# A router worked in two groups of token tiles, and three weight matrices held until the first gathered rows have landed

## The reference

```python
def hier_moe(hn, w_group, w_expert, w_gate, w_up, w_down):
    t = hn.reshape(-1, d)
    pg = jax.nn.softmax((t @ w_group).astype(jnp.float32), axis=-1)
    g_sel = jnp.argmax(pg, axis=-1)
    ...
    el_sel = jnp.take_along_axis(el, g_sel[:, None, None], axis=1)[:, 0]
    top_p, top_i = lax.top_k(jax.nn.softmax(el_sel, axis=-1), TOP_K_IN_GROUP)
    w = p_sel * top_p / jnp.sum(top_p, axis=-1, keepdims=True)
    ...
    for e in range(N_EXPERTS):
        a = jax.nn.silu(t @ w_gate[e]) * (t @ w_up[e])
        out = out + comb[:, e:e + 1] * (a @ w_down[e]).astype(jnp.float32)
```

## Time and profile before

| | us |
|---|---|
| median of 3 runs | 558.82 |
| lowest, highest | 556.86, 560.46 |
| the profiled execution | 559.13 |
| its span | 557.3 |

### The profile page before, as it was taken

The page is one execution under the profiler, slowest core; times in us unless marked ns, Lnnn a source line. Parts: engine busy times, 40 slices in busy tenths (PEclk is TensorE's granted clock), DMA queues, the critical chain, the costliest instruction groups (busy, mean ns, idle before and its releaser), DMA issues.

```text
span 557.3 us, 7527 instructions
## 1 busy us (share of the span) xinstructions
PE 489.2 (88%) x2747; PEld 309.0 (55%) x2747; DVE 267.8 (48%) x595; ACT 132.7 (24%) x361; POOL 155.8 (28%) x279
## 2 busy tenths in 40 slices
PE   4968989899999989899992999979999789787985
PEld 3946767677776767688882754333433233333333
DVE  2869679878464475752227423223342221122535
ACT  3744455356446223222111100000000000000110
POOL 4354783042113555823004300111112210100003
PEclk9998999799999999899997699989999998898998
DMA  9430220040029703249939989999999999999997
GB/s 296 161 109 23 76 76 2 1 152 1 2 81 319 272 8 98 86 162 411 388 141 403 339 316 376 410 422 417 422 418 420 419 418 420 421 419 421 413 384 268
DMA packets 35030, 144.73 MB, mean 260 GB/s; under 512 B 5842, under 2 KB 8994, under 8 KB 23216
## 3 DMA queue, kind: packets, MB, share of 16 engines
q1 hardware_dynamic: 26320, 129.94, 59.4%
q0 software_dynamic: 4528, 9.01, 4.4%
q10 hardware_dynamic: 4144, 5.28, 2.9%
HBM read 138.16 MB, written 17.30 MB: 279 GB/s over the span
## 4 chain that ended last, share of the span: by engine, by line
PE 38%; DMA 20%; DVE 15%; SPq 11%; issue 6%; ACT 4%; POOL 1%; DVEq 0%; POOLq 0%; ACTq 0%
PE banks L1061 17%; SPq L724 7%; PE banks L1326 5%; DMA y_d<-y_sb,idx 5%; DMA w_moe_b<-in_w_up_dram 5%; DMA y_d<-rows,idx 3%; SPq L732 3%; DMA w_moe_b<-y_d 2%; DMA y_d<-x_row,idx 2%; PE banks L1416 1%; DMA y_sb<-hn_d,idx 1%; PE banks L1276 1%; PE banks L1123 1%; ACT w_hi L1604 1%; PE banks L1341 1%
## 5 line engine op out<-in xcount | busy, mean ns | idle before, releaser
L882 POOL TENSOR_TENSOR w_lo<-w_raw,w_hi 128x512 fp32r<-128x512 f32 x52 | 70.1, 1363 | 113.8 <-ACT w_hi L1604 112.4
L1326 PE MATMUL banks<-w_moe_b,xgT 128*64 128x512 f32 x224 | 68.8, 637 | 10.3 <-DMA w_moe_b<-in_w_up_dram 6.6
L1326 PE MATMUL banks<-w_moe_a,xgT 128*64 128x512 f32 x224 | 67.7, 626 | 5.6 <-DMA w_moe_a<-in_w_up_dram 5.6
L2270 DVE SCALAR_TENSOR_TENSOR glu_b<-banks,wr,glu_a 128x256 f32<-128x256 f32 x15 | 7.2, 483 | 99.5 <-ACT glu_a L1736 99.5
L1736 ACT ACTIVATE glu_a<-banks,wr 128x256 f32<-128x256 f32 x15 | 7.1, 473 | 200.1 <-PE banks L1326 185.7
L1061 PE MATMUL banks<-w_hi,xT_hi_a 128*128 128x512 f32 (+3 forms) x124 | 51.3, 414 | 2.8 <-DVE xT_lo_a L1798 2.8
L1326 PEld LDWEIGHTS banks<-w_moe_b,xgT 128*64 128x64 f32 x224 | 21.7, 145 | 49.8 <-issue 49.1
L1061 PE MATMUL banks<-w_lo,xT_hi_a 128*128 128x512 f32 (+3 forms) x124 | 49.1, 396 | 0.0
L1061 PE MATMUL banks<-w_hi,xT_lo_a 128*128 128x512 f32 (+3 forms) x124 | 48.8, 393 | 0.0
L1326 PEld LDWEIGHTS banks<-w_moe_a,xgT 128*64 128x64 f32 x224 | 21.4, 144 | 27.2 <-issue 27.0
L1061 PE MATMUL banks<-w_hi,xT_hi_b 128*128 128x512 f32 (+3 forms) x92 | 35.7, 388 | 0.4 <-issue 0.4
(11 more groups left out here) (336 smaller groups left out, 910.9 us busy)
## 6 DMA issues: line engine op xcount, KB each, us to landing
w_moe_a<-in_w_down_dram SPq DMA_DIRECT2D x20, 1024.0 KB, 21.0
w_moe_a<-in_w_gate_dram SPq DMA_DIRECT2D x16, 1024.0 KB, 12.4
w_moe_a<-in_w_up_dram SPq DMA_DIRECT2D x16, 1024.0 KB, 14.8
w_moe_b<-in_w_gate_dram SPq DMA_DIRECT2D x14, 1024.0 KB, 18.2
w_moe_b<-in_w_up_dram SPq DMA_DIRECT2D x14, 1024.0 KB, 18.3
w_moe_b<-in_w_down_dram SPq DMA_DIRECT2D x10, 1024.0 KB, 26.5
w_raw<-in_w_in_dram SPq DMA_DIRECT2D x34, 256.0 KB, 4.0
y_d<-in_consts_dram SPq DMA_DIRECT2D x9, 512.0 KB, 10.1
```

The lines of the kernel that those rows point to most:

```text
L882: nc.gpsimd.tensor_tensor(w_lo[:, s, :], w_raw[:, s, :], w_hi[:, s, :].bitcast(F32), ALU.subtract).then_inc(split, 1)
L1326: l = mm(acc[64 * e:64 * e + 64, u, :].rearrange("p (m f) -> p m f", m=2), xgT[:, xu, k, 64 * e:64 * e + 64], units(at_e[e], 2)[:, :, k * ...
L2270: stt(out=glu_b[:, :], in0=acc[:, u, 0:FF], scalar=scales[0], in1=glu_a[:, :], op0=ALU.mult, op1=ALU.mult).then_inc(done, 1)
```

## The change

The router's block is split. The first three tiles of `ORDER` (tile 4, 0 and 1; `AHEAD` = 3) are chosen in a step `choose` that the plan puts between the last jobs of `OUT1`; `logits`, `ssq2` and the table of destinations are now laid out by position in `ORDER`. TensorE's ranks for these three (`ranks_ahead`, three products) stand inside the very last job, ahead of its last matrix; DVE's `rank_in`, `rows_picked` and `rows_placed` stand among the last evictions. The block after the plan does the same for the remaining two tiles: the choice, two products that carry the first group over (one of them with `ahead_sum`) and two more, and rows. `find_rows` for the indices is taken apart: six of its ten products need only the first group. The two steps that make `ms`, and the signal `ms2_rdy` that POOL waits for, move from ahead of the choice to behind the last `row_oh`. One memset of POOL (128 x 768) is dropped, since its memory now serves as scratch.

In SP's queue `gate_v[5]` and `down_v[5]` (pair 2's second expert) and `down_v[0]` move behind the wait for the first gathered rows, where `down_v[1]` already stood.

```diff
@@ -63,6 +63,8 @@
 OUT0 = len(CHUNKS)
 OUT1 = OUT0 + 1
 NJ = NT * (OUT0 + 2)
+AHEAD = 3
+RANK_BANK = 5
...
@@ -185,6 +187,12 @@
             after[s + 1].append(("hT", n, t))
             after[s + 2].append(("logit", n, t))
 
+    last = at[OUT1, ORDER[-1], 0]
+    after[last - 1].append(("choose",))
+    before[last + 1].append(("rank_in",))
+    after[last + 1].append(("rows_picked",))
+    after[last + 2].append(("rows_placed",))
...
@@ -276,7 +288,7 @@
     put("ret_scale", np.concatenate([q_scale, k_scale], -1).transpose(1, 0, 2))
     head = 2 * np.arange(2)[None, :] + (p[:, None] >= 64)
     put("decay", np.stack([gamma[head] ** n for n in (P, DEC, NMETA)], 1))
-    tok = np.arange(NT)[None, :] * P + p[:, None]
+    tok = np.asarray(ORDER)[None, :] * P + p[:, None]
...
@@ -783,16 +794,15 @@
             sp.dma_start(units(gu_unit(3, 0) + 1, 1)[:, 0, :], up_v[6]).then_inc(gu_in[3], 16)
             sp.wait_ge(acc_done, NJ)
             load_gu_of(2, 0)
-            sp.dma_start(units(gu_unit(2, 1), 1)[:, 0, :], gate_v[5]).then_inc(gu_in[2], 16)
-            sp.dma_start(dn_at(2, 1), down_v[5]).then_inc(dn_in[2], 16)
 
             sp.wait_ge(hn_out, 16 * NT)
             sp.wait_ge(hT_ps, 2 * NT)
             sp.wait_ge(sq2, 2 * NT)
 
-            sp.dma_start(dn_at(0, 0), down_v[0]).then_inc(dn_in[0], 16)
             sp.wait_ge(xg_in[0], 16)
-            sp.dma_start(dn_at(0, 1), down_v[1]).then_inc(dn_in[0], 16)
+            load_dn(0)
+            sp.dma_start(units(gu_unit(2, 1), 1)[:, 0, :], gate_v[5]).then_inc(gu_in[2], 16)
+            sp.dma_start(dn_at(2, 1), down_v[5]).then_inc(dn_in[2], 16)
             sp.wait_ge(gate_ps, 1)
             load_gu_of(3, 1)
             sp.wait_ge(gu_ps, 1)
...
@@ -909,7 +919,7 @@
 
             pool.wait_ge(acc_done, NJ)
 
-            for n, of in enumerate((y_sb[:, 1, 2 * NT * P - D:], x_row[DEC:, 0, :], rows[:, :, :])):
+            for n, of in enumerate((x_row[DEC:, 0, :], rows[:, :, :])):
                 nc.gpsimd.memset(of, 0.0).then_inc(rows_clear, 1)
                 pool.wait_ge(rows_clear, n + 1)
...
@@ -1009,6 +1019,17 @@
                 l.then_inc(xt_ps, 1)
                 busy[b] = [(xt_part, n)]
 
+            def ranks_ahead():
+
+                pe.wait_ge(m_ready, 1)
+                take(RANK_BANK)
+                mm(side3[:, 0:NE * AHEAD], counting[:, 0, :], chosen[:, 0:AHEAD, :].rearrange("p t e -> p (t e)"),
+                   start=True, stop=False)
+                for s in range(1, AHEAD):
+                    l = mm(side3[:, NE * s:NE * AHEAD], counting[:, 1, :],
+                           chosen[:, 0:AHEAD - s, :].rearrange("p t e -> p (t e)"), start=False, stop=(s == AHEAD - 1))
+                l.then_inc(rank_ps, 1)
+
             def job(c, t, half, b):
 
                 i = ORDER.index(t)
...
@@ -1039,6 +1060,8 @@
                         pe.wait_ge(rm_hi, 2 * i + 2)
                         pe.wait_ge(rm_lo, 2 * i + 2)
                 for kk in range(4 * half, 4 * half + 4):
+                    if j == NJ - 1 and kk == KD - 1:
+                        ranks_ahead()
...
@@ -1286,29 +1309,36 @@
                     does[kind](*args)
 
 
-            pe.wait_ge(m_ready, 1)
+            def find_row(c, table, oh_rows, j, start, stop):
+                return mm(found[:, c:c + 2 * NPAIR], oh_rows[:, j, :], table[:, j, :], start=start, stop=stop)
+
+            def find_rows(c, table, oh_rows):
+                for j in range(2 * NT):
+                    l = find_row(c, table, oh_rows, j, j == 0, j == 2 * NT - 1)
+                return l
+
+            pe.wait_ge(m_ready, 2)
             for b in range(SIDES):
                 take(b)
-
-
-            mm(side3[:, 0:NE * (NT + 1)], counting[:, 0, :], chosen[:, :, :].rearrange("p t e -> p (t e)"),
+            mm(side3[:, NE * AHEAD:NE * (NT + 1)], counting[:, 0, :], chosen[:, AHEAD:, :].rearrange("p t e -> p (t e)"),
                start=True, stop=False)
-            for s in range(1, NT + 1):
-                l = mm(side3[:, NE * s:NE * (NT + 1)], counting[:, 1, :],
-                       chosen[:, 0:NT + 1 - s, :].rearrange("p t e -> p (t e)"), start=False, stop=(s == NT))
+            mm(side3[:, NE * AHEAD:NE * (NT + 1)].rearrange("p (t e) -> p t e", e=NE), counting[:, 1, :],
+               ahead_sum[:, :].unsqueeze(1).to_broadcast([P, NT + 1 - AHEAD, NE]), start=False, stop=False)
+            for s in range(1, NT + 1 - AHEAD):
+                l = mm(side3[:, NE * (AHEAD + s):NE * (NT + 1)], counting[:, 1, :],
+                       chosen[:, AHEAD:NT + 1 - s, :].rearrange("p t e -> p (t e)"), start=False, stop=(s == NT - AHEAD))
             l.then_inc(rank_ps, 1)
-
-            def find_rows(c, table, oh_rows, half=None):
-
-                for j in range(2 * NT):
-                    if half is not None and j % NT == 0:
-                        pe.wait_ge(half, j // NT + 1)
-                    l = mm(found[:, c:c + 2 * NPAIR], oh_rows[:, j, :], table[:, j, :], start=(j == 0),
-                           stop=(j == 2 * NT - 1))
-                return l
+            pe.wait_ge(oh_ready, 2)
+            for k in range(2):
+                for i in range(AHEAD):
+                    find_row(0, pair_dst, row_oh, NT * k + i, k == 0 and i == 0, False)
+            pe.wait_ge(oh_ready, 3)
+            for k in range(2):
+                for i in range(AHEAD, NT):
+                    l = find_row(0, pair_dst, row_oh, NT * k + i, False, k == 1 and i == NT - 1)
+            l.then_inc(idx_ps, 1)
 
             pe.wait_ge(x2_add, 2 * NT)
-            find_rows(0, pair_dst, row_oh, oh_ready).then_inc(idx_ps, 1)
 
             for _ in range(9):
...
+            def choose_of(lo, n, r32, cand, el, el2, oh_e):
...
+                step(red(col(30), gl, AX_X, ALU.max))
+                step(tt(r4[:, of, :], gl, wide(col(30), NG), ALU.subtract))
+                step(stt(out=cand[:, :, 0:NG], in0=r4[:, of, :], scalar=0.0, in1=iota_n(NG), op0=ALU.is_equal, op1=ALU.mult))
+                lowest(groups, cand[:, :, 0:NG], NG)
+                e4 = logits[:, of, NG:].rearrange("p t (g e) -> p t g e", g=NG)
+                step(tt(r32, e4, groups.unsqueeze(3).to_broadcast([P, n, NG, EPG]), ALU.mult))
+                step(red(el, r32.rearrange("p t g e -> p t e g"), AX_X, ALU.add))
+                step(red(col(35), el, AX_X, ALU.max))
...
+                    step(tt(oh[:, k, of].rearrange("p t (g e) -> p t g e", g=NG),
+                            oh_e[:, k].unsqueeze(2).to_broadcast([P, n, NG, EPG]),
+                            groups.unsqueeze(3).to_broadcast([P, n, NG, EPG]), ALU.mult))
+                if lo == 0:
+                    step(nc.vector.memset(oh[DEC:, :, 0, :], 0.0))
+                step(tt(chosen[:, of, :], oh[:, 0, of], oh[:, 1, of], ALU.add))
+                if lo == 0:
+                    two, by_tile = scratch[:, 504:504 + NE], [chosen[:, i, :].bitcast(F32) for i in range(AHEAD)]
+                    step(tt(two, by_tile[0], by_tile[1], ALU.add))
+                    step(tt(ahead_sum[:, :], two, by_tile[2], ALU.add))
+                dve.sem_inc(m_ready, 1)
+
+            def rank_of(lo, n, rank1):
+
+                ranks = side3[:, NE * lo:NE * (lo + n)].rearrange("p (t e) -> p t e", t=n)
+                step(tt(rank1, ranks, const("pair_row1").unsqueeze(1).to_broadcast([P, n, NE]), ALU.add))
...
+                step(stt(out=rank1, in0=ranks, scalar=float(CAP), in1=rank1, op0=ALU.is_lt, op1=ALU.mult))
+
+            def rows_by_kind(lo, n):
+                return row_l[:, :].rearrange("p (k t) -> p k t", k=2)[:, :, lo:lo + n]
+
+            def pick_of(lo, n, rank1, tmp):
+
+                step(tt(tmp, oh[:, :, lo:lo + n, :], rank1.unsqueeze(1).to_broadcast([P, 2, n, NE]), ALU.mult))
+                step(red(rows_by_kind(lo, n), tmp, AX_X, ALU.add))
+
+            def place_of(lo, n):
+
+                return tt(row_oh[:, :, :].rearrange("p (k t) s -> p k t s", k=2)[:, :, lo:lo + n, :],
...
+                n = int(np.prod(shape))
+                of = scratch[:, lo:lo + n]
+                if len(shape) == 2:
+                    return of.rearrange("p (a b) -> p a b", a=shape[0])
+                return of.rearrange("p (a b c) -> p a b c", a=shape[0], b=shape[1])
+
...
+
+            def choose(b):
+                dve.wait_ge(lg_ev, nth["logit", 1, ORDER[AHEAD - 1]])
+                choose_of(0, AHEAD, lot(0, AHEAD, NG, EPG), lot(96, AHEAD, EPG), lot(120, AHEAD, EPG), lot(144, AHEAD, EPG),
+                          lot(168, 2, AHEAD, EPG))
+
+            def rank_in(b):
+                dve.wait_ge(rank_ps, 1)
+                rank_of(0, AHEAD, ahead_rank)
+
+            def rows_picked(b):
+                pick_of(0, AHEAD, ahead_rank, ahead_tmp)
+
+            def rows_placed(b):
+                place_of(0, AHEAD).then_inc(oh_ready, 1)
 
```

(54 more changed lines are left out.)

70 lines of the change are left out of this document (38 added, 32 removed).

## The result

| | before | changed |
|---|---|---|
| median of 20 runs, us | 558.21 | 561.13 |
| lowest, highest, us | 556.25, 560.93 | 558.35, 564.28 |
| profiled execution, us | 559.13 | 560.01 |
| its span, us | 557.3 | 558.2 |

The ratio to before is 1.0044, 95% interval 1.0025 to 1.0064: 2.5 us slower, inside one per cent. The forecast was 559.6, 0.8 us over before, with 555.5 to 564: the measured time lies inside that range, and the slowdown is about three times the one forecast.

A forecast was written before the change was run, and what follows sets the result against it. The end was taken as set by the bytes left once the DMA's full stretch begins. Router -2.8 us, taken back by POOL's root; backlog +0.5, TensorE +0.8, the later counting: +0.8, 559.6 us on the median, range 555.5 to 564.

The forecast's parts named there:

- The bound: Last stretch, from 348 us: bytes left set the end, not any engine; 7.5 us of transfer time lost at 312-338.
- The router: Router in two groups: part ahead costs 1.4 us, idx at 306.2 against 309.0, a gain of 2.8 us.
- The root: POOL's root, behind the late ms steps, ends at 309.0; first gather starts where now, taking back the 2.8 us.
- The hold: SP's matrices held for the first gather: the DMA's hole moves from 312-338 to 305-314, 7.3 us lost against 7.5.
- the backlog: DMA works off everything queued by pair 4's release at 335.7 against 335.2: +0.5 us (0.2 earlier to 2.0 later).
- TensorE's clock: After nine idle products TensorE waits 2.2 us and may stay at its lower clock: +0.8 us, ends -0.3 and +2.6.
- the later counts: In the sum, the later of DMA backlog (+0.5 us) and TensorE (+0.8 us) moves the end: +0.8 us.
- (a): Rival: POOL's root does not hold the gather, which starts at 307.1; -2.3 us, about 556.5; chance 0.15.
- (b): Rival: TensorE at the lower clock from 309.9 through the first pair's first half; about 561.5 to 564; chance 0.25.
- (c): Rival: the DMA's hole really closes, gather landing near 309 and TensorE warm; -5 us or more, 553.5; chance 0.06.

The follow-up runs named there:

- e3: Changed kernel with only the two ms steps and their signal moved back ahead of the second group's choice; ratio to before 0.9992.
- e2: Kernel before, router in one piece, with only SP's order of the change (three more matrices held until the first gather has landed); ratio to before 1.0054.
- e7: Changed kernel with thirteen idle products on TensorE instead of nine; ratio to before 1.0037.
- e1: Changed kernel without the hold: SP's queue as before, router still split and ms steps late; ratio to before 1.0054.
- e10: Changed kernel, ms steps late, with gate 5 and down 5 let go, only down 0 and down 1 held; ratio to before 1.0028.
- e11: Changed kernel with ms steps early and only down 0 and down 1 held, a repeat run of that kernel; ratio to before 0.9994.
- e4: Changed kernel with the ms steps moved back early and SP's order as before the change; ratio to before 1.0031.
- e8: Changed kernel with ms steps early and SP's held loads waiting for idx_ready instead of the first gather; ratio to before 1.0044.
- e9: Kernel before, router in one piece, with down 0 alone moved behind the wait for the first gather; ratio to before 0.9974.
- e12: Same kernel as e9 once more (router in one piece, down 0 moved behind the wait); ratio to before 0.9981.

## Why the prediction was right or wrong, point by point

**The bound.** Right. Over fourteen profiled executions the rest of the span follows the lost transfer time, from 265.9 us at 5.4 lost to 273.8 at 12.8, none more than 0.8 us off a straight line. As all fourteen move the same matrices, this says mainly that little more is lost, or won back, after the 102 us of the ruler; what makes the loss is shown by the experiments.

**The router.** Right in its parts. Choice ahead 5.6 us forecast, 5.8 measured (285.15 to 290.93); delay of the last logits 1.4 forecast, 1.7 measured; gain at idx 2.8 forecast, 2.5 measured. The second group's choice was forecast at 4.75 us from its start to m_ready and took 4.64 (296.32 to 300.96).

**The root.** Right, and shown: the gather's start was forecast where it was before, it started 0.3 us earlier, and e3, which moves two steps of DVE, brings it forward and the time down by 0.5%.

**The hold.** The mechanism was right (the hole moves and does not close), the size was not. The term that was mis-sized is the backlog: "landing at 313.0 ... bytes flow from 314.4 ... 7.3, against 7.5 now". The queue ran dry as forecast, 15.8 us from the zero (forecast 16.05; 3 GB/s from 304 on), but two other parts were off. The gather in a dry queue took 4.0 to 4.2 us, not 3.3 (changed kernel, e2, e3, e7); that is the upper half of the stated 2.6 to 4.8, and the 2.7 us estimated from the Trainium skill's fit ("DMA: Bandwidth & Descriptors", "Anatomy of one DMA") is further off still. And behind the gather the queue did not jump to 422 GB/s: it moved 287 GB/s from 311 to 318 and 329 from 313 to 321, with the engines busy 0.86 and 0.92 of the time, so another 1.8 us were lost after bytes had begun to flow. Gathers and first matrices share the queue there; which of them keeps the rate down was not tested. On the ruler the change loses 1.4 us more than before, e2 1.9 more. The prediction had two figures for this one term, 0.2 us less by loss and +0.5 us by the end of the backlog, and its sum used the second; both are too small.

**TensorE's clock.** The forecast added +0.8 us because "the later counts". TensorE was late by 1.0 us at pair 4's loads (46.1 against 45.1), as forecast, but it did not count; the backlog did, with some 2 us, and the sum of 0.8 came out right in sign for the wrong term, which is luck. e7 took 2.9 us of that lateness away and gained nothing that shows. The level itself fell: granted 0.91 of full speed under the twenty products (2.82 us), then 0.50 from 313 to 319, under the transposes (1.95 us) and the first pair's 32 products (5.63 us, 4.71 before). TensorE would have counted without the hold, as in e1 and e10.

**The rivals.** (a), an early gather, did not happen in the change; e3 made it and it was worth 2.9 us against the change (1.0044 to 0.9992), but that is level with before where (a) had -2.3: the hold goes on costing. (b), TensorE at the lower clock through the first pair, had 561.5 to 564, and 561.1 came: by the number it was the nearest, and the lower clock did come, but e7 shows that it was not what was paid. What (b) describes is e1, at 5.3 us in its profiled execution and 3.0 in its ratio; it is a price of the late root. (c) was out of reach: the best trace (e11) still lost 5.4 us. The Trainium skill's rule that engines take turns between queues ("DMA: Bandwidth & Descriptors", "Queues, rings and completion order") was held against the hold; the waits of this gather, 6.5 us in e4 and 8.8 in e8, do not come out of it as a share of the time.

**What stays open.** Whether the split router is worth anything at all once down 0 is held too: the means of the two kernels differ by 0.02%, which these runs know to about 0.3%. What makes e4 0.3% slower than before. Whether the part ahead, which takes 1.7 us of the router's 4.2 back, could be hidden was not tried.

## What to carry to other kernels

When a ring of transfers sets the end, price a change by the time in which the queue stands dry, not by the engine time that it saves: a hold ahead of a small urgent transfer pays only as far as the queue would still be full when that transfer is issued. Here holding one matrix more was right (0.2% faster, e9 and e12) and three more were too many (0.5% slower, e2). Ask of every step that is moved what waits behind it on the other engine too: two steps of 0.2 us, put behind the critical chain to shorten it, held POOL's root, and the root held the gather for which the chain had been shortened.

## What the runs showed of the hardware that I had not expected

- A gather of 72 or so rows (0.29 MB) takes 4.0 to 4.2 us in a dry queue, 4.8 behind the queue of before with down 0 as its last matrix, 6.5 when it is issued 1.6 us sooner behind the same queue (e4), and 8.8 when 4 MB are issued 0.9 us ahead of it (e8). Behind one and the same queue its landing hardly moves with its issue: 25.8, 25.9 and 26.1 us from the zero for issues at 21.0, 19.4 and 21.5.
- Four more idle products cost 0.45 us in all (4.19 to 4.64 us), because the granted clock rose during them (mean 0.67 against 0.50), and the 60 instructions behind them ran 2.8 us faster (10.3 us from the start of find_rows to the issue that the first pair's gate releases, against 7.5); between two profiled executions of one and the same kernel the same stretch differs by 0.5 us.
